# Two transformer blocks on one core: x and the scale halves first in the opening, a merged norm before the first feed-forward, and two reordered attention stages

## The reference

```python
c_act = silu(c)
mod = c_act @ w_ada + b_ada                      # 1 x 6144
sh1, sc1, gt1, sh2, sc2, gt2 = split(mod, 6)
h = rmsnorm(x, g_mix) * (1 + sc1) + sh1
x = x + gt1 * mixer(h, ...)                      # two-way mLSTM and pooling, then w_out
h = rmsnorm(x, g_ffn) * (1 + sc2) + sh2
x = x + gt2 * (square(relu(h @ w_ff1)) @ w_ff2)
x = rmsnorm(x, g_final)
# second block: SSD mixer and MLA attention beside each other, gates, w_o, then a gated feed-forward
h = rms_norm(x, norm_mix_g)
x = x + (g_ssd * y_ssd + g_mla * y_mla) @ w_o
x = x + (silu(u_gate) * u_val) @ w_down          # u = conv(rms_norm(x) @ w_up)
```

## Time and profile before

| what | us |
|---|---|
| median of 3 runs | 1689.63 (1689.29 to 1690.36) |
| the profiled execution | 1689.39 |
| its span in the profile | 1687.6 |
| TensorE busy | 1655.1 (98% of the span) |
| VectorE busy | 1116.7 (66%) |
| ScalarE busy | 720.3 (43%) |
| GpSimd busy | 119.2 (7%) |
| TensorE's granted clock | 1.00 |

### The profile page before, as it was taken

One profiled execution on the slowest core, in us unless ns is written; L12 is line 12 of the kernel. 1 busy time (PEld: TensorE's weight loads), 2 busy tenths in 40 slices (PEclk: granted clock), 3 DMA queues, 4 the chain that ended last, 5 costly groups with the idle time before them and its releaser, 6 DMA issues.

```text
span 1687.6 us, 20002 instructions
## 1 busy us (share of the span) xinstructions
PE 1655.1 (98%) x7797; PEld 1316.6 (78%) x7797; DVE 1116.7 (66%) x1423; ACT 720.3 (43%) x1002; POOL 119.2 (7%) x128
## 2 busy tenths in 40 slices
PE   6999999999999999999999999999999999999999
PEld 3888777888888887887666788886578888888887
DVE  2888866532454577787999974538878786642364
ACT  3443323221222235646888523538742364431242
POOL 0005100000000000000233200003400000000000
PEclk9999999999999999999999999999999999999999
DMA  9554321222222242222111222221022222222222
GB/s 384 194 196 176 128 81 69 100 100 100 100 91 89 96 150 76 100 75 100 50 51 51 77 98 98 69 100 51 1 100 100 95 87 94 99 100 100 100 101 100
DMA packets 25422, 174.18 MB, mean 103 GB/s; under 512 B 2800, under 2 KB 3184, under 8 KB 5104
## 3 DMA queue, kind: packets, MB, share of 16 engines
q1 hardware_dynamic: 21440, 146.52, 24.3%
q10 hardware_dynamic: 3888, 26.38, 3.9%
HBM read 168.69 MB, written 4.19 MB: 102 GB/s over the span
## 4 chain that ended last, share of the span: by engine, by line
PE 81%; DVE 13%; ACT 3%; issue 2%; DMA 1%; ACTq 0%; SPq 0%; DVEq 0%; POOL 0%
PE bank L1559 25%; PE bank L1560 25%; PE bank L1561 25%; DVE p L1255 3%; DVE w_lo L846 2%; ACT p L377 1%; PE bank L2095 1%; DVE clipped L1231 1%; DMA x<-x_in 1%; PE bank L1771 1%; PE bank L1697 1%; PE bank L1753 1%; DVE xbc L1223 1%; DVE t L943 1%; PE bank L1605 1%
## 5 line engine op out<-in xcount | busy, mean ns | idle before, releaser
L1559 PE MATMUL bank<-h,w_hi 128*128 128x512 f32 x1200 | 472.5, 394 | 5.1 <-DVE w_lo L846 2.2
L1561 PE MATMUL bank<-h,w_lo 128*128 128x512 f32 x1200 | 467.2, 389 | 0.0
L1560 PE MATMUL bank<-h,w_hi 128*128 128x512 f32 x1200 | 467.1, 389 | 0.0
L377 ACT ACTIVATE w_hi<-raw 128x2048 fp32r<-128x2048 f32 (+1 forms) x129 | 246.6, 1912 | 327.5 <-DMA raw<-slabs 322.9
L846 DVE TENSOR_TENSOR w_lo<-raw,w_hi 128x2048 fp32r<-128x2048 f32 (+1 forms) x129 | 296.6, 2300 | 89.6 <-ACT w_hi L377 85.7
L1559 PEld LDWEIGHTS bank<-h,w_hi 128*128 128x128 f32 x1200 | 225.3, 188 | 55.5 <-DVE w_lo L846 3.5
L1560 PEld LDWEIGHTS bank<-h,w_hi 128*128 128x128 f32 x1200 | 225.3, 188 | 47.5 <-issue 1.4
L1561 PEld LDWEIGHTS bank<-h,w_lo 128*128 128x128 f32 x1200 | 225.2, 188 | 47.1
L1559 PE MATMUL bank<-a_hi,w_hi 128*128 128x512 f32 x432 | 168.1, 389 | 0.3 <-DVE x L1493 0.3
L1561 PE MATMUL bank<-a_hi,w_lo 128*128 128x512 f32 x432 | 168.1, 389 | 0.0
L1560 PE MATMUL bank<-a_lo,w_hi 128*128 128x512 f32 x432 | 168.0, 389 | 0.0
(11 more groups left out here) (340 smaller groups left out, 2341.6 us busy)
## 6 DMA issues: line engine op xcount, KB each, us to landing
raw<-slabs SPq DMA_DIRECT2D x127, 1024.0 KB, 4.8
ada_chunk<-ada ACTq DMA_DIRECT2D x24, 1024.0 KB, 7.0
x<-x_in SPq DMA_DIRECT2D x4, 1024.0 KB, 9.4
spill_x<-x SPq DMA_DIRECT2D x1, 2048.0 KB, 11.6
x<-spill_x SPq DMA_DIRECT2D x2, 1024.0 KB, 7.0
out<-x SPq DMA_DIRECT2D x8, 256.0 KB, 2.0
raw<-slabs SPq DMA_DIRECT2D x2, 768.0 KB, 4.5
inv<-inv ACTq DMA_DIRECT2D x1, 1024.0 KB, 6.9
```

The costliest lines, as they stand in the source:

```text
L377: return act.activation(out, in_, f, **kw)
L1559: pe.matmul(out, w[0], a[0], start=start, stop=False)
L1560: pe.matmul(out, w[0], a[1], start=False, stop=False)
L1561: return pe.matmul(out, w[1], a[0], start=False, stop=stop)
```

## The change

1. **Opening.** SyncE loads the first half of x, ScalarE the second as its first issue. The chunks of the first third come as halves: eight issues for the scale columns (`scale_in0`, `scale_in1`, four chunks each), then eight for the shift columns (`ada_in0` to `ada_in7`). TensorE sums the squares first, then eight scale halves (two parts each, bank 4), turns them, then eight shift halves (bank 3) with five fillers after each of chunks 3 to 6, and turns those. VectorE makes all eight scaled tiles in a buffer of their own before the shifts are ready; then ScalarE and VectorE only add the shift and split. SyncE's wait before slab 1 moves from chunk 6 to chunk 7.
2. **Merge before `ff1a`.** `out` also produces u2 = x * gain (high and low part, L900's operation) and `ff1a` starts with `product_from_unscaled`, totals after k = 0, root spread after k = 1. The fillers go. The shift's share of the first two result tiles is made by `shift_product` inside the last tile of `out`: 32 matmuls with two moving columns. `first_tiles` scales the two tiles, and ScalarE applies relu with the shift as bias, in place. `modulated(2)` starts with `weight_tail(slab + 1)`; ScalarE rounds slab 2 of `ff1a` in the middle of its heads. The last third of the modulation moves to the first slab of `out`.
3. **State space projection.** The fourth `turn_heads` of each group moves from k = 12 to k = 14.
4. **Attention.** VectorE's loop goes by pairs of heads, with reciprocals between the maxima, and the split of `ao` moves to GpSimd, after its scaling of every odd head (the last pair stays on VectorE).
5. Semaphores of the two softplus chains are renamed and shared, and one that nobody waits for is gone.

```diff
-            for k in range(0, KT, 4):
-                sp.dma_start(x[:, k:k + 4, :], x_d[:, k:k + 4, :]).then_inc(sem("x_in"), 16)
+            sp.dma_start(x[:, 0:4, :], x_d[:, 0:4, :]).then_inc(sem("x_in"), 16)
...
-                    sp.wait_ge(sem("ada_in6"), 16)
+                    sp.wait_ge(sem("ada_in7"), 16)
...
+            act.dma_start(x[:, 4:8, :], x_d[:, 4:8, :]).then_inc(sem("x_in"), 16)
             for n in range(KT):
-                ada_load(n)
+                act.dma_start(ada_chunk[n][:, KT * P:], ada_d[n, :, KT * P:]).then_inc(sem(f"scale_in{n // 4}"), 16)
+            for n in range(KT):
+                act.dma_start(ada_chunk[n][:, 0:KT * P], ada_d[n, :, 0:KT * P]).then_inc(sem(f"ada_in{n}"), 16)
...
+            for k in range(KT):
+                do.tell(dve.scalar_tensor_tensor(scaled[:, k, :], x[:, k, :], gain[:, k:k + 1], rs[:], ALU.mult, ALU.mult),
+                        "h_scaled", k + 1)
+            dve.wait_ge(sem("mod_done"), 1)
+            mod_half(banks[3], SH1)
...
-            for n in range(2):
-                mod_chunk(n)
             sum_squares(KT, sq)
-            for n in range(2, KT):
-                mod_chunk(n)
-                if n in (4, 5, 6):
+            for n in range(KT):
+                mod_chunk(n, 1)
+            pe.wait_ge(sem("consts_in"), 16)
+            pe.wait_ge(sem("scale_row"), 1)
+            half_turn(banks[4]).then_inc(sem("scale_turned"), 1)
+            for n in range(KT):
+                mod_chunk(n, 0)
+                if n in (3, 4, 5, 6):
                     kept_busy(banks[6], 5)
...
+                        if (n, m) == (3, 1):
+                            shift_product(k)
                     last.then_inc(sem("tile_done"), 1)
 
-            kept_busy(banks[3], 14)
-            total_square(1)
-            kept_busy(banks[3], 5)
-            spread_root(1)
-            kept_busy(banks[3], 16)
+            product_from_unscaled("ff1a", (u2_hi, u2_lo), (h_hi, h_lo), 2, lambda: total_square(1), 0, 1)
...
+                for j in range(2 * k % KT, 2 * k % KT + 2):
+                    for part, w in enumerate(weights(slab, KT * m + j)):
+                        last = pe.matmul(banks[3][:, 2 * m:2 * m + 2], w, shift_parts[:, j, :], start=j + part == 0,
+                                         stop=j == KT - 1 and part == 1)
...
-                        if k:
+                        if 0 < k < 12:
                             turn_heads(n - 1)
+                    if t in (2, 4) and k == 14:
+                        turn_heads(2 * (t - 2) + 3)
...
+            for hd in range(0, QH, 2):
+                totals_inverted(hd, 0)
+                if hd:
+                    copy_tail(hd - 1)
+                maxima(hd + 1, (0, 1))
+                totals_inverted(hd, 1)
+                maxima(hd + 1, (2, 3))
+                totals_inverted(hd + 1, 0)
+                if hd:
+                    take_pair(hd // 2 - 1)
+                totals_inverted(hd + 1, 1)
+                copy_tail(hd)
+                if hd + 2 < QH:
+                    maxima(hd + 2)
...
+                if hd >= 3 and hd % 2:
+                    pair = (hd - 3) // 2
+                    pool.wait_ge(sem("pair_taken"), pair + 1)
+                    do(pool.tensor_copy(att[:, 2 * pair, :], ao[:]))
+                    do.tell(pool.tensor_tensor(att[:, 2 * pair + 1, :], ao[:], att[:, 2 * pair, :].bitcast(f32), ALU.subtract),
+                            "att_made", pair + 1)
```

More of the change, by code:

```diff
@@ L426, in norm, with heads @@
                 root(rs)
-            def heads(stage, shift=None, place=h_hi):
+            def heads(stage, shift=None, place=h_hi, between=None):
                 for k in range(KT):
+                    if between is not None and k == 4:
+                        between()
                     n = KT * (stage - 1) + k + 1
@@ L562, in _ @@
                 do.tell(fn(y_hi[:, head, :], (t0, t1)[head % 2][:], ACT.Copy, scale=half_gain[:, head:head + 1]), "y_head", head + 1)
[L563 to L566, removed]
+            mod_copy(2, banks[6])
+            weight_head(SLAB0["out"] + 2)
+            for n in range(3, 6):
+                for m in range(2 * n - 6, 2 * n - 4):
+                    unscaled_head(2, m, u2_hi, gain[:, KT + m:KT + m + 1], ("bank_free", FREED["out"]))
+                weight_head(SLAB0["out"] + n)
+            for m in range(6, 8):
+                unscaled_head(2, m, u2_hi, gain[:, KT + m:KT + m + 1], ("bank_free", FREED["out"]))
             root(rs, totals=1)
-            heads(2, SH2)
+            heads(2, SH2, between=lambda: weight_head(SLAB0["ff1a"] + 2))
+            root_copy(1)
             for half, name in enumerate(("ff1a", "ff1b")):
@@ L930, in modulated @@
                 spread = rs
+                if stage == 2:
+                    weight_tail(slab + 1)
                 if stage > 1:
@@ L957, in modulated @@
                     do.tell(ins, "h_ready", first + k + 1)
-                    if stage == 2 and k == 3:
-                        weight_tail(slab + 1)
-                if stage > 2:
+                if stage > 1:
                     weight_tail(slab + 2)
@@ L1664, in mod_turn, with mod_chunk, half_turn @@
                 last.then_inc(sem("mod_done"), 1)
-            def mod_chunk(n):
-                pe.wait_ge(sem(f"ada_in{n}"), 16)
-                for part in range(4):
-                    last = pe.matmul(banks[4][32 * part:32 * part + 32, :], c_act[:, n:n + 1].to_broadcast([P, 32]),
-                                     ada_chunk[n][:, S * part:S * part + S], start=n == 0, stop=n == KT - 1)
-                last.then_inc(sem("ada_used"), 1)
+            def mod_chunk(n, half):
+                if half:
+                    pe.wait_ge(sem(f"scale_in{n // 4}"), 64)
+                else:
+                    pe.wait_ge(sem(f"ada_in{n}"), 16)
+                for part in range(2):
+                    first = S * (2 * half + part)
+                    last = pe.matmul(banks[3 + half][32 * part:32 * part + 32, :], c_act[:, n:n + 1].to_broadcast([P, 32]),
+                                     ada_chunk[n][:, first:first + S], start=n == 0, stop=n == KT - 1)
+                last.then_inc(sem("scale_used" if half else "ada_used"), 1)
+            def half_turn(bank):
+                for m in range(4):
+                    last = pe.transpose(bank[:, 64 * m:64 * m + 64], mod_row[0:64, P * m:P * m + P], ident[0:64, 0:64])
+                return last
             def tile(name, t):
```

187 lines of the change are left out of this document (113 added, 74 removed).

## The result

The changed kernel takes 1694.68 us (median of 8 runs, 1694.34 to 1695.75) against 1689.49 (8 runs, 1688.91 to 1691.24): ratio 1.0031, 95% interval 1.0020 to 1.0042. It is slower by 5.2 us; the forecast was 1685.7, with 1681 to 1692 as the range. The profiled execution has a span of 1692.5 us at a granted clock of 1.0.

The account below looks back on a forecast made before the run. TensorE was taken as the bound (busy 1655.1 of 1687.6 us). Opening +5.4, merge -4.4, state space -0.9 and attention -4.0 sum to -3.9 against the profiled 1689.4: 1685.5, adjusted to the median 1685.7, range 1681 to 1692.

Parts of the forecast that it names:

- The step that failed: Opening: ScalarE's 17 issues at 0.52 us each take 8.8 us, so squares start at 11.1; part of the opening's +5.4 us.
- my bounds: Opening: price per ScalarE issue; 0.41 us would make the opening +3.5 us, 0.585 would make it +6.5.
- the rival that it costs half: Opening: half a chunk costs 0.46 us instead of 0.90, taking 7 us off, for 1678.7 us; chance 0.10.
- The transfers themselves aren't late: Opening: same bytes in flight, and TensorE reaches the last shift half near 41 us, against chunk 7 done at 36.2 before.
- The merge: From `out` to tile 4 of `ff1a`: -4.4 us, with bounds -7.8 to -3.3; chance that it returns nothing 0.10.
- the wait for relu at the end: Merge: TensorE waits 2.1 us for VectorE's relu that frees bank 0, the new last wait there.
- The 32 small matmuls: Merge: `shift_product`'s two-column matmuls in `out` add 3.4 us, with bounds from nothing to 4.5.
- My three waits: Merge: TensorE waits of 0.5, 1.1 and 2.1 us, taken as too short to slow its clock; counted as nothing.
- State space: State space projection: moving the fourth turn two k steps later removes its 0.48 us wait and its twin's: -0.9 us.
- Attention: Attention: without the split on VectorE, pairs of heads go from 9.6 to 8.9 us: -4.0 us; chance of nothing 0.15.
- 9.3 a pair: Attention: VectorE's maxima and reciprocals about 3.7 us twice, copy 0.7, split 1.15; 8.1 without the split, making TensorE the bound.
- The rival of slow GpSimd: Attention: GpSimd's copy and subtraction take 3.2 us each, pairs go to 10.5 us, +7.8 instead of -4.0: 1697.5; chance 0.08.

Follow-up runs that it names:

- e8: Changed kernel, but ScalarE issues the eight shift halves behind the last square instead of behind the scale halves: 1685.35 us, ratio 0.9974.
- e2: Changed kernel with six of each eight halves as two transfers of three chunks, 9 ScalarE issues instead of 17, same pieces: 1694.1 us, ratio 1.0028.
- e10: Kernel before the change, with chunk 7 brought in by eight transfers of 16 partitions, 15 ScalarE issues, same 1024 pieces: 1695.89 us (one run).
- e4: Changed kernel with the old opening's whole chunks, but x leading on both queues and squares ahead of all chunk sums: 1677.43 us, ratio 0.9926.
- e6: Kernel before the change, chunks 0 to 5 as three pairs in 4 KB pieces: 8 transfers, 1792 pieces instead of 1024; 1691.31 us (one time).
- e1: Changed kernel with the eight shift halves issued on SyncE's queue, behind slab 0, instead of ScalarE's: 1692.37 us, ratio to before 1.0017.
- e11: e8 without the 20 fillers among the shift sums and with 9 instead of 14 at the end: 1683.24 us, ratio 0.9965.
- e9: Changed kernel with the old opening, attention's split back on VectorE, new order kept: 1678.95 us, against 1678.99 with the split on GpSimd.

## Why the prediction was wrong

**The step that failed** is in the opening: "I take 0.52, nearer to the first since these issues too run beside SyncE's: 8.8 us from 0.74". It took a price from eight issues and used it for 17. Nothing in the trace of before shows a tenth issue in a row, so the price had a lower bound but no upper one; my bounds, 0.41 to 0.585, were both of a queue with room. The 17 issues took 18.4 us instead of 8.8. The whole miss, 1694.7 less 1685.7, is 9.0 us; taking the standing away (e8) gives back 9.3 and lands at 1685.35. No rival had it, and the slow side of the range, 1692, was too near for that reason. The experiments say what fills: a queue takes only so many pieces that aren't yet worked off, with neither transfers (e2, e10) nor bytes (e4, e6) to blame. At how many it begins isn't settled, nor whether it is the same for larger pieces. In after the first long issue is the one that makes 1280 in all, 1.17 us, and clearly the one at 1536, 2.98 us; in e2 and e6 the one that made 1536 went in within the usual time and the next stood for 6 us; on SyncE's queue in e1 it is the one at 1408, 1.84 us.

**The rest of the opening held, with two errors that cancel.** Half a chunk costs 0.88, so the rival that it costs half fell. In e8 the squares start with x at 10.25 (11.1 forecast) and the first product at 46.11 (46.0). The forecast followed VectorE to the first tile of h and left out the 14 fillers that TensorE runs behind the last turn; in e8 as in after they end 1.0 us behind that tile. "The transfers themselves aren't late" held there too, but not once both queues carry them (e1).

**The merge, -5.6 against -4.4.** `out` ended 2.2 us later relative to the first product (268.70 less 250.92, less 15.6) where 2.5 was forecast, and from the last addition to tile 4 it is 26.7 instead of 27.6. The mis-sized term is the wait for relu at the end, forecast 2.1 and in the trace 0.78. The 32 small matmuls: 3.4 taken, and 3.15 for 29 of them measured. h stayed ahead of TensorE. My three waits lay under 1 us (0.53, 0.78, 0.78) and no dip of the clock followed. So they didn't try the rule of the Trainium skill ("TensorE: Matmul & The Clock Gate", its part on the HAM clock gate) that idleness brings the array to half rate. It shows elsewhere: granted clock 0.50 after waits of 5.55 us (e1) and 2.29 us (e11).

**State space, -1.4 against -0.9.** The 0.48 us waits are gone (1076.80 has no idle before it). The rest wasn't followed up.

**Attention, -4.1 against -4.0, with a cause that wasn't needed.** The sum was right because TensorE's 8.96 is the floor under either story. I put VectorE's work at 9.3 a pair and concluded that the split must go. That 9.3 took 3.7 for each head, a figure that holds a wait of 0.77 which only one head of a pair has, and left out the two copies of 0.42 to `pt`; busy time is 8.27. e9 shows that order alone does it. That taking off the split alone would have done it too is an estimate (8.45), not a run. The rival of slow GpSimd did not come about: its cast took 0.61 and its subtraction 1.28 us on average, and its load is useless here rather than harmful.

## What to carry to other kernels

A price for an issue holds only for as many pieces as the trace shows in a row: count the pieces (partitions times rows of a transfer), not the bytes alone, before a compute engine issues more than it did, and put what isn't needed yet behind that engine's first work. Splitting a transfer in two to get one half early doubles the pieces, and here also TensorE's passes. When an engine looks full, take its waits out of the sum before you move work off it: here a change of order alone gave what a second engine was brought in for.

## What was not expected of the hardware

- An issue on ScalarE's queue took 0.45 to 0.6 us as a rule, and up to 6.83 us with 1536 to 2048 pieces issued; the engine did nothing else meanwhile. SyncE's queue did the same in e1 (up to 2.72 us, from 1408 pieces on).
- Eight transfers of 16 partitions and 128 KB each ran the DMA engines at 135 to 168 GB/s (e10, 30 to 36 us), against 420 with 1 MB transfers.
- A wait of 2.29 us behind nine fillers was followed by a granted clock of 0.50 in e11, while waits of 0.8 us, and the 2.14 us in the earlier trace rows, were followed by nothing.
